# Two-layer diffusion block on one core: steps of the last pair, a later weight load, and operands on 128 bytes

## What is computed

```python
z = u_lat @ w_in                                                # even layer
y_a = z[AB] * _dwconv(z[AC] * z[AX], w_conv, 1) * silu(z[AG])
y_b = _neighbourhood_attention(q, k, v, k_c, v_c, rpb) * silu(z[BG])
h = h + gate * (concatenate([y_a, y_b]) @ w_out)                # 2048 x 1024
x = _dwconv(z[:W_RNN], conv_w, 1) + conv_b                      # odd layer, W_RNN = 2048
r, i = sigmoid(blockdiag(x, w_ra) + b_ra), sigmoid(blockdiag(x, w_ri) + b_ri)   # 2 directions
a = exp(8 * r * log_sigmoid(lam)); b = sqrt(-expm1(2 * log_a)) * i * x
y = forward_scan(a0, b0) + backward_scan(a1, b1)
h = h + gate * ((y * silu(z[W_RNN:])) @ w_out)
out = _rmsnorm(h, final_g)
```

## Time and profile before

| | us |
|---|---|
| runs, median of 3 | 2343.79 (2342.88 to 2345.22) |
| the profiled execution, its time | 2341.55 |
| its span, first to last instruction | 2339.7 |
| mean granted TensorE clock | 0.990 |

### The profile page before, as it was taken

One profiled execution on the slowest core, in us unless ns is written; L12 is line 12 of the kernel. 1 busy time (PEld: TensorE's weight loads), 2 busy tenths in 40 slices (PEclk: granted clock), 3 DMA queues, 4 the chain that ended last, 5 costly groups with the idle time before them and its releaser, 6 DMA issues. The chain is left out here.

```text
span 2339.7 us, 33518 instructions
## 1 busy us (share of the span) xinstructions
PE 2256.0 (96%) x11996; PEld 1961.3 (84%) x11996; DVE 1506.2 (64%) x2407; ACT 1166.4 (50%) x1712; POOL 481.8 (21%) x287
## 2 busy tenths in 40 slices
PE   6999999999999999999998899799999999999998
PEld 4788888888888888888886688699999999998786
DVE  4576675765757657576566436648667866776755
ACT  4534445345353453444434234347876787678311
POOL 0232231322313223132220020021122112210000
PEclk9999999999999999999999999899999999999999
DMA  7121221112221111221133656201111111113521
GB/s 290 40 55 47 65 62 64 54 51 66 59 67 54 52 62 53 66 65 52 56 113 92 210 148 179 88 27 54 62 47 54 54 52 57 54 54 126 209 80 63
DMA packets 146665, 187.50 MB, mean 80 GB/s; under 512 B 50520, under 2 KB 109144, under 8 KB 143448
## 3 DMA queue, kind: packets, MB, share of 16 engines
q1 hardware_dynamic: 138888, 166.67, 22.8%
q10 hardware_dynamic: 7632, 18.88, 2.2%
HBM read 155.62 MB, written 29.88 MB: 79 GB/s over the span
## 5 line engine op out<-in xcount | busy, mean ns | idle before, releaser
L1372 PE MATMUL ps<-u_hi,w_hi 128*128 128x512 f32 (+1 forms) x1464 | 532.9, 364 | 0.0
L1372 PE MATMUL ps<-u_hi,w_lo 128*128 128x512 f32 (+1 forms) x1464 | 519.0, 354 | 0.0
L1372 PE MATMUL ps<-u_lo,w_hi 128*128 128x512 f32 (+1 forms) x1464 | 517.8, 354 | 0.0
L1372 PEld LDWEIGHTS ps<-u_hi,w_lo 128*128 128x128 f32 x1464 | 276.2, 189 | 40.0
L1372 PEld LDWEIGHTS ps<-u_lo,w_hi 128*128 128x128 f32 x1464 | 277.0, 189 | 35.1
L1372 PEld LDWEIGHTS ps<-u_hi,w_hi 128*128 128x128 f32 x1464 | 276.4, 189 | 35.2
L2301 PE MATMUL ps<-u_hi,o_w_hi 128*128 128x426 f32 (+2 forms) x640 | 239.9, 375 | 9.8 <-POOL o_w_lo L1876 9.4
L727 ACT ACTIVATE probs<-probs,neg_max 128x640 f32<-128x640 f32 (+1 forms) x160 | 122.8, 767 | 248.4 <-DVE neg_max L1050 248.4
L2301 PE MATMUL ps<-u_lo,o_w_hi 128*128 128x426 f32 (+2 forms) x640 | 239.2, 374 | 0.0
L2301 PE MATMUL ps<-u_hi,o_w_lo 128*128 128x426 f32 (+2 forms) x640 | 239.1, 374 | 0.0
L635 POOL TENSOR_TENSOR bias_tile<-bias_piece,col_mask 128x384 f32<-128x384 f32 x128 | 141.2, 1107 | 455.8 <-DVE neg_max L1050 455.7
(11 more groups left out here) (247 smaller groups left out, 4610.3 us busy)
## 6 DMA issues: line engine op xcount, KB each, us to landing
w_stage<-in_w_even SPq DMA_DIRECT2D x63, 512.0 KB, 3.9
o_w_raw<-in_w_odd SPq DMA_DIRECT2D x48, 512.0 KB, 3.8
ada_piece<-in_w_ada SPq DMA_DIRECT2D x20, 1024.0 KB, 5.8
y_raw<-y_scratch SPq DMA_DIRECT2D x40, 512.0 KB, 5.5
wout_raw<-in_w_out SPq DMA_DIRECT2D x16, 512.0 KB, 6.9
y_scratch<-h_backward SPq DMA_DIRECT2D x16, 512.0 KB, 3.2
final_w_raw<-in_w_out SPq DMA_DIRECT2D x8, 1024.0 KB, 11.2
final_y_raw<-y_scratch SPq DMA_DIRECT2D x15, 512.0 KB, 4.6
```

The lines of the kernel that those rows point to most:

```text
L1372: last = nc.tensor.matmul(ps[:, bank(j, g), 0:t - f], w[:, slot, c * P:(c + 1) * P], x[:, c, f:t], start=(c == 0 and n == 0), stop=(c == K ...
```

## The change

- `GROUPS` and `QGROUPS` go from three nearly equal groups to 512/512/rest.
- `Map.align()` moves the next tile to a multiple of 128 bytes. It stands before the q stack (`x_at`), before `probs`, before `o_w_hi`, and before `x_hi`; the rows of `x_hi` and `x_lo` are padded to 1312 columns.
- In the last pair, unit 8 moves to step 5 and units 10 and 11 to steps 7 and 8; tiles 0 to 3 start in steps 9, 12, 15 and 19. The hooks move with them, and a third hook, `ahead(s)`, stands between the units and copy_low or output.
- The second weights are loaded in pairs behind the halves of tiles 5 to 8, and split after tiles 6 to 9 in place of 5 to 8.

```diff
-GROUPS = [(0, 428), (428, 854), (854, 1280)]
+GROUPS = [(0, 512), (512, LAT), (LAT, TOK)]
+    def align(self):
+        self.at = (self.at + P - 1) // P * P
-LAST_UNITS = ((0,), (1,), (2, 3), (4,), (5, 6), (7,), (8, 9), (10, 11))
+LAST_UNITS = ((0,), (1,), (2, 3), (4,), (5, 6), (7, 8), (9,), (10,), (11,))
-OUT_CHUNKS = {8: (0, 0, 5), 9: (0, 5, 11), 10: (0, 11, YC), 11: (1, 0, 5), 12: (1, 5, 11), 13: (1, 11, YC),
-              14: (2, 0, 5), 15: (2, 5, 10), 16: (2, 10, 13), 17: (2, 13, YC), 18: (3, 0, 4), 19: (3, 4, 8)}
+OUT_CHUNKS = {9: (0, 0, 5), 10: (0, 5, 11), 11: (0, 11, YC), 12: (1, 0, 5), 13: (1, 5, 11), 14: (1, 11, YC),
+              15: (2, 0, 5), 16: (2, 5, 9), 17: (2, 9, 13), 18: (2, 13, YC), 19: (3, 0, 4)}
     raw_v = m("raw_v", [P, TOK + 4])
+    m.align()
     x_at = Map.BASE + m.at
     convw = m("conv_w", [P, 24])
+    m.align()
     prob_at = Map.BASE + m.at
@@ sync
-                for q in range(4):
-                    load_out_w(1, q)
                 load_x(0, 4, 0)
                 for t in range(5, NT):
                     load_tile(0, t, t % 2)
+                    if t < 9:
+                        load_out_w(1, t - 5)
@@ vector, hooks of the last pair (scalar has the same order with out_w_hi, out_y_hi)
             within: s == 7: out_w_lo(0), out_w_lo(1)
-              8: out_w_lo(3), out_y_lo(0,0,1)   9: out_w_lo(5)   10: out_w_lo(7)   11: out_y_lo(1,1,1)
-              13: out_y_lo(2,0,1), first_half(0)   15: first_half(1)   17: out_y_lo(3,1,1)
+              8: out_w_lo(2)   9: out_w_lo(4)   10: out_y_lo(0,0,1), out_w_lo(6)   12: out_y_lo(1,1,1)
+              14: first_half(0)   16: first_half(1)
+            ahead:  8: out_y_lo(0,0,0)
             behind:
-              7: out_y_lo(0,0,0), out_w_lo(2)   8: out_w_lo(4)   9: out_w_lo(6)   10: out_y_lo(1,1,0)
-              11: gate_diagonal(0,0)   12: out_y_lo(2,0,0)   14: gate_diagonal(0,1)   16: out_y_lo(3,1,0)
+              8: out_w_lo(3)   9: out_w_lo(5)   10: out_w_lo(7)   11: out_y_lo(1,1,0), gate_diagonal(0,0)
+              13: out_y_lo(2,0,0)   14: out_y_lo(2,0,1)   15: gate_diagonal(0,1)   16: out_y_lo(3,1,0)
+              17: out_y_lo(3,1,1)
@@ scalar, projection()
-                    if 5 <= t < 9:
-                        out_w_hi(2 * t - 2)
-                        out_w_hi(2 * t - 1)
+                    if t >= 6:
+                        out_w_hi(2 * t - 4)
+                        out_w_hi(2 * t - 3)
@@ odd layer
-QGROUPS = [(0, 428), (428, 856), (856, QCOLS)]
+QGROUPS = [(0, 512), (512, LAT), (LAT, QCOLS)]
+XCOLS = 1312
+    m.align()
     WHI_AT = m.at
-    xhi, xlo = m("x_hi", [P, 2, QCOLS], F32R), m("x_lo", [P, 2, QCOLS], F32R)
+    m.align()
+    xhi, xlo = m("x_hi", [P, 2, XCOLS], F32R), m("x_lo", [P, 2, XCOLS], F32R)
```

More of the change, by code:

```diff
@@ L863, in body @@
                             project(i, j, g, last)
+                    if last:
+                        ahead(s)
                     copy_low(i, s)
@@ L911, in within, with ahead, behind @@
                 elif s == 8:
+                    out_w_hi(2)
+                elif s == 9:
+                    out_w_hi(4)
+                elif s == 10:
+                    out_y_hi(0, 0, 1)
+                    out_w_hi(6)
+                elif s == 12:
+                    out_y_hi(1, 1, 1)
+            def ahead(s):
+                if s == 8:
+                    out_y_hi(0, 0, 0)
+            def behind(s):
+                i = PAIRS - 1
+                if s == 6:
+                    act.wait_ge(ya_done, i + 1)
+                    store_conv(act, i, 0, LAT // 2)
+                elif s == 8:
                     out_w_hi(3)
-                    out_y_hi(0, 0, 1)
+                    act.wait_ge(ya_done, i + 3)
+                    store_conv(act, i, LAT // 2, LAT)
+                    store_conv(act, i, LAT, TOK)
                 elif s == 9:
@@ L918, in within @@
                 elif s == 11:
[L919 to L925, removed]
-                i = PAIRS - 1
-                if s == 6:
-                    act.wait_ge(ya_done, i + 1)
-                    store_conv(act, i, 0, LAT // 2)
[L931 to L935, removed]
-                    act.wait_ge(ya_done, i + 3)
-                    store_conv(act, i, LAT // 2, LAT)
-                    store_conv(act, i, LAT, TOK)
-                elif s == 9:
-                    out_w_hi(6)
-                elif s == 10:
                     out_y_hi(1, 1, 0)
@@ L944, in behind @@
                     copy_gate_row(0)
+                elif s == 13:
                     out_y_hi(2, 0, 0)
                 elif s == 14:
+                    out_y_hi(2, 0, 1)
+                elif s == 15:
                     store_half(0)
@@ L950, in behind @@
                     out_y_hi(3, 1, 0)
+                elif s == 17:
+                    out_y_hi(3, 1, 1)
                     store_half(1)
@@ L1163, in within, with ahead, behind @@
                 elif s == 8:
+                    out_w_lo(2)
+                elif s == 9:
+                    out_w_lo(4)
+                elif s == 10:
+                    out_y_lo(0, 0, 1)
+                    out_w_lo(6)
+                elif s == 12:
+                    out_y_lo(1, 1, 1)
+                elif s == 14:
+                    first_half(0, half_link)
+                elif s == 16:
+                    first_half(1, half_link)
+            def ahead(s):
+                if s == 8:
+                    out_y_lo(0, 0, 0)
+            def behind(s):
+                if s == 8:
                     out_w_lo(3)
-                    out_y_lo(0, 0, 1)
                 elif s == 9:
@@ L1170, in within @@
                 elif s == 11:
[L1171 to L1189, removed]
                     out_y_lo(1, 1, 0)
-                elif s == 11:
                     dve.wait_ge(ya_stored, 32 * PAIRS + 16)
                     gate_diagonal(0, 0).then_inc(diag_done, 1)
-                elif s == 12:
+                elif s == 13:
                     out_y_lo(2, 0, 0)
                 elif s == 14:
+                    out_y_lo(2, 0, 1)
+                elif s == 15:
                     gate_diagonal(0, 1).then_inc(diag_done, 1)
@@ L1199, in behind @@
                     out_y_lo(3, 1, 0)
+                elif s == 17:
+                    out_y_lo(3, 1, 1)
             def out_a(pass_, t, b, i):
@@ L1915, in x_hi @@
                     act.wait_ge(gate_mm, n * 24 + 24)
-                nc.scalar.activation(xhi[:, mm, :], xc[:, mm, :], ACT.Copy).then_inc(xhi_done, 1)
+                nc.scalar.activation(xhi[:, mm, 0:QCOLS], xc[:, mm, :], ACT.Copy).then_inc(xhi_done, 1)
             def tanh_z(n, j, g):
@@ L2095, in x_low @@
                 dve.wait_ge(xhi_done, 2 * n + (2 if mm else 3))
-                nc.vector.tensor_tensor(xlo[:, mm, :], xc[:, mm, :], xhi[:, mm, :].bitcast(F32),
+                nc.vector.tensor_tensor(xlo[:, mm, 0:QCOLS], xc[:, mm, :], xhi[:, mm, 0:QCOLS].bitcast(F32),
                                         ALU.subtract).then_inc(xlo_done, 1)
```

## The result

The changed kernel takes 2328.09 us (median of 4 runs, 2326.4 to 2329.8) against 2343.34 us (2342.05 to 2345.22) for the kernel before, in runs side by side: ratio 0.9934, 95% interval 0.9917 to 0.9952. That is -15.2 us where -9.4 was forecast; the time lies inside the range, 6.3 us under the forecast. The profiled execution has a span of 2326.2 us against 2339.7, 13.56 us less.

A forecast was written before the change was run, and what follows sets the result against it. TensorE, busy 96% of the span, was taken as the bound. Terms -9.2 - 5.2 + 2 + 0 + 2 + 1 = -9.4 us took 2341.55 to 2332.15; with 2.24 to the median, 2334.4 us, range 2322 to 2341.

The forecast's parts named there:

- Second weights: Pass 0, tile 5: loads moved behind tiles 5 to 8 remove its 6.56 us wait and 2.66 at 1.2 GHz; -9.2 us.
- the cover: First tile of pass 1: last two pieces ready at +6.0 and +8.6 us, needed at +8.3 and +9.7; 1.1 us spare.
- Last pair: Last pair's steps: waits 11.3 us against 15.2, loss at 1.2 GHz 2.3 against 3.6; -5.2 us, bounds 0 and -12.
- X groups: Odd layer, projected groups of 512/512/256: a set takes 14.06 to 14.24 us against 14.01; +2 us, between +0.8 and +3.7.
- Gates: Odd layer, LRU gates: 36 matmuls stay at 7.01 us; 0, with -4 if all matched and +4 if all mismatched.
- Pass 1: Output projection's pass 1: distance between matmuls rises from 228.9 to 233.3 ns; +2 us (matched -1).
- odd against even: One operand on an odd, the other on an even multiple of 128 bytes: 233.3 ns a matmul, against 226.7 both odd.
- Attention: Value stack and probabilities come to stand odd against even, in 704 matmuls of 256 columns; +1 us, 0 to +3.
- Rival A: Layout does nothing, distances follow columns, so all layout terms are 0: 2329.4 us, chance 0.18.
- Rival B: Multiples of 128 bytes are what counts: X, gates and pass 1 fall to 226.7 ns; 2320 us, chance 0.08.
- C: Last pair gains nothing, as VectorE's list is only rearranged and the stalls come back: 2339.6 us, chance 0.12.
- D: Slower: y halves of tiles 6 to 9 come late behind 1 MB of weights each; 2352.8 us, chance 0.04.

The follow-up runs named there:

- load_only: Kernel before with only the second weights' loads moved behind the halves of tiles 5 to 8, splits to tiles 6 to 9: 2332.15 us against 2342.23.
- groups_only: Kernel before with only the odd layer's groups changed, to 512/512/256 and 512/512/260, at the old addresses: 2342.32 us against 2342.23.
- align_only: Kernel before with only the four alignments and the padded x_hi and x_lo, groups as before: 2342.21 us against 2342.23.
- same_place: Changed kernel with other addresses alone: stationary and moving operands agree modulo 256 bytes, in the attention the moving one 64 ahead: 2329.36 us.

## Why the prediction was right or wrong, point by point

1. *Second weights: right.* -6.57 from tile 4 to tile 5 and -2.66 behind it, forecast 6.56 + 2.66. Both terms had been read off this same trace of before, so the agreement says that the wait went whole; what was open was the cover. The last two pieces' splits end 8.61 us after the start of pass 1, forecast +8.6, and nothing waits:

```profile
1375.29 5.34 POOL L675 TENSOR_TENSOR wout_lo<-wout_raw,wout_hi 128x1024 fp32r<-128x1024 f32 x2 [7.33 <-ACT wout_hi L892]
```

2. *Last pair: the mechanism right, one term wrong in sign.* New waits forecast 2.2 + 2.8 + 4.1 + 2.2 = 11.3, measured (start to start, less the usual step) 2.46 + 2.09 + 3.55 + 2.42 = 10.5, at just these places and none before tile 2, the wait for probs_t and the two for y operands ended by VectorE, and that before tile 0 too by the times above. But the loss at 1.2 GHz was to fall from 3.6 to 2.3 us and rose instead, by 1.6 (by 1.1 to 1.3 against load_only and groups_only); so -2.2 in place of -5.2, or -3.5 to -4.0 against those two traces. The working took the loss as a share of the waits, and this is the step that failed: the waits fell and the time at the low clock rose. That it goes by how close together they stand is argued, not shown. The attention was to end some 8 us earlier and ended 2.7 us earlier (last weigh 1299.39 and 1296.67).

3. *X groups: wrong.* 14.00 us a set, forecast 14.06 to 14.24, and 14.04 with the groups alone. The addresses were wrong (and `o_w_lo`, 96 past a multiple of 128, was left out), and the 256-column unit took 118.7 ns a matmul, where 119.6 to 127 was taken. About 0 in place of +2.

4. *Gates: mis-sized.* 6.97 us against 7.01: 32 sets, -1.4 in place of 0. With the Z units (32, 11.15 against 11.19 for two: -0.6) that is the block's 78.19 us in place of 78.50, about -2.2. The rest of the odd layer's -3.5 doesn't come from the change: 0.5 us up to the first gates and 0.6 in the last block are missing in load_only too, whose odd layer is that of before. Parts 3 and 4 said +2: the largest miss, -5.5 by the traces and -4.3 without that rest.

5. *Pass 1: right in size, for a reason that needed mending.* +1.6, forecast +2; a first tile takes 11.19 us, forecast 11.20. Moving weights at 0 and y at 128 modulo 256 are out of place; the "odd against even" of the forecast is the same thing here.

6. *Attention: +1.8 in pairs 0 to 6,* forecast +1, bounds 0 to +3; align_only shows +2.1, same_place +0.5.

Not in the sum: *the final products,* -2.3. From the fifth tile on all take 10.88 us (the first four are interleaved), as the y buffers and both halves of the weights now stand in the same place. The forecast said that it would be wrong if tiles 5 and 6 lost their difference, and there it was. It had no term for this because of the wrong address.

Together: the forecast's -9.4 and the trace's -13.6 differ by +3.0 (part 2), -5.5 (parts 3 and 4), -2.3 (final), and +0.8 in parts 5, 6 and the prologue: -4.0, and 0.2 of rounding. The medians put the gain 1.6 us higher still; the trace of before is of an execution, 2341.55 us, under all four runs timed beside the change. That the time fell inside the range is in part luck: the last pair's miss and those of the layout point opposite ways. Rival A's 2329.4 is nearest to the time, yet its reason falls: places matter by up to 7 ns a matmul, and what they cost and gave in this kernel (+1.8, +1.6, -3.5, -2.3) sums to -2.4, or to -1.2 with load_only's odd layer for before. Rival B fails on its premise: a difference of 128 bytes is as slow as one of 32. C (2339.6) and D (2352.8) didn't happen; the y halves of tiles 6 to 9 were there in time.

## What to carry to other kernels

Before a layout is argued from addresses, take them from the program itself, not from a sum, and measure the pace of the bare instruction over all places once. A wait removed from TensorE is worth more or less than its length: count the slow instructions behind it, and try filling it. Before a stage's distances are added up against one trace, look at a second execution of the same code. Where one engine is 99% busy, look at how long before its need the other engines' results are ready: here it was 0.33 us a block, and matmuls up to 6 ns shorter brought nothing.

## What the runs showed of the hardware

- Start to start of 128 x 128 x 512 fp32r matmuls at the full clock: for places that are multiples of 32, 226.7 to 228.3 ns where stationary and moving operand start at the same place modulo 256 bytes, 228.8 to 229.4 with the moving one 64 bytes ahead, 232 to 234 at the others. Off the multiples of 32 it was 227.0 to 237.1, and 230.1 with both operands 16 on. Traffic of VectorE and ScalarE in SBUF doesn't change it by more than 0.1 ns. In a triple of hi and lo parts, one part of the stationary operand out of place costs as much as both (234.8 against 233.4).
- 256 columns took 113.3 to 120.0 ns by place, 260 columns 118.5 to 121.1, and 128 columns still 109.5 to 111.8: half the columns save less than a tenth of the time.
- In this kernel VectorE and GpSimd blocked each other until the other's instruction ended: a 1.50 us product took 3.57 behind a 2.54 us split, and a 0.69 us scan 2.91.
